# The last three even output tiles in two passes, latents first, and the odd norm's latent chain under the second

## The reference, cut to what matters

```python
for i in range(DEPTH):                                  # DEPTH = 2
    update_ctx = i < DEPTH - 1
    h_lat = rms_norm_2(x_lat, norm_g[i]) * (1.0 + sc_l) + sh_l
    h_ctx = rms_norm_2(x_ctx, norm_g[i]) * (1.0 + sc_c) + sh_c
    y_lat, y_ctx = even_mixer(h_lat, h_ctx, ...) if i == 0 else odd_mixer(h_lat, h_ctx, ...)
    x_lat = x_lat + g_l * y_lat
    if update_ctx:
        x_ctx = x_ctx + g_c * y_ctx
return rms_norm_2(x_lat, final_g)
```

## Time and profile before

| | |
|---|---|
| median of 3 runs | 2489.65 us |
| the profiled execution, its own time | 2498.05 us |
| its span | 2496.3 us |
| PE, DVE, ACT busy | 97%, 66%, 44% |
| chain that ended last | PE 86%, DVE 8%, ACT 3%, issue 2% |
| granted TensorE clock, mean of the span | 0.991 |

### The profile page before, as it was taken

The page is one execution under the profiler, slowest core; times in us unless marked ns, Lnnn a source line. Parts: engine busy times, 40 slices in busy tenths (PEclk is TensorE's granted clock), DMA queues, the critical chain, the costliest instruction groups (busy, mean ns, idle before and its releaser), DMA issues.

```text
span 2496.3 us, 36288 instructions
## 1 busy us (share of the span) xinstructions
PE 2423.2 (97%) x14094; PEld 1960.7 (79%) x14094; DVE 1655.3 (66%) x3206; ACT 1100.0 (44%) x2073; POOL 0.2 (0%) x4
## 2 busy tenths in 40 slices
PE   8999999999999999999999999999999999999998
PEld 6878888778888778788887888887866666878766
DVE  6767577474447776674865644488586677489765
ACT  4346355443232243464544423333446667242563
POOL 0000000000000000000000000000000000000000
PEclk9999999999999999999999999999999999999999
DMA  4320143223337522201522333465110000122211
GB/s 155 96 76 28 40 139 96 73 79 99 94 100 236 176 75 91 68 20 51 169 68 68 93 97 97 152 219 164 60 43 18 18 18 18 60 77 68 81 47 60
DMA packets 61802, 217.68 MB, mean 87 GB/s; under 512 B 6976, under 2 KB 9280, under 8 KB 60864
## 3 DMA queue, kind: packets, MB, share of 16 engines
q1 hardware_dynamic: 48384, 176.06, 22.8%
q10 hardware_dynamic: 13248, 39.29, 4.7%
HBM read 213.23 MB, written 2.10 MB: 86 GB/s over the span
## 4 chain that ended last, share of the span: by engine, by line
PE 86%; DVE 8%; ACT 3%; issue 2%; ACTq 0%; DMA 0%; DVEq 0%
PE bank L614 21%; PE bank L615 20%; PE bank L616 20%; PE bank L878 4%; PE bank L916 3%; PE bank L890 3%; DVE w_lo L576 2%; PE bank L645 1%; PE bank L647 1%; PE bank L646 1%; ACT w_hi L569 1%; PE bank L671 1%; DVE e_s L991 1%; PE bank L1522 1%; PE bank L673 1%
## 5 line engine op out<-in xcount | busy, mean ns | idle before, releaser
L569 ACT ACTIVATE w_hi<-w_raw 128x1024 fp32r<-128x1024 f32 x334 | 353.7, 1060 | 552.3 <-PE bank L616 505.8
L576 DVE TENSOR_TENSOR w_lo<-w_raw,w_hi 128x1024 fp32r<-128x1024 f32 x334 | 407.9, 1223 | 232.7 <-ACT w_hi L569 231.7
L614 PE MATMUL bank<-a_hi,w_hi 128*128 128x512 f32 x1344 | 535.0, 398 | 20.4 <-DVE w_lo L576 18.5
L616 PE MATMUL bank<-a_hi,w_lo 128*128 128x512 f32 x1344 | 526.1, 391 | 0.0
L615 PE MATMUL bank<-a_lo,w_hi 128*128 128x512 f32 x1344 | 525.7, 391 | 0.0
L614 PEld LDWEIGHTS bank<-a_hi,w_hi 128*128 128x128 f32 x1344 | 252.3, 188 | 83.0 <-issue 18.7
L616 PEld LDWEIGHTS bank<-a_hi,w_lo 128*128 128x128 f32 x1344 | 252.0, 188 | 55.7
L615 PEld LDWEIGHTS bank<-a_lo,w_hi 128*128 128x128 f32 x1344 | 252.5, 188 | 51.7 <-issue 1.0
L614 PE MATMUL bank<-b_hi,w_hi 128*128 128x512 f32 x440 | 182.5, 415 | 4.0 <-DVE w_lo L576 2.7
L615 PE MATMUL bank<-b_lo,w_hi 128*128 128x512 f32 x440 | 172.9, 393 | 0.0
L616 PE MATMUL bank<-b_hi,w_lo 128*128 128x512 f32 x440 | 172.3, 392 | 0.0
(11 more groups left out here) (465 smaller groups left out, 4412.0 us busy)
## 6 DMA issues: line engine op xcount, KB each, us to landing
w_raw<-w_tiles SPq DMA_DIRECT2D x334, 512.0 KB, 3.5
mod_raw<-mod_tiles ACTq DMA_DIRECT2D x48, 512.0 KB, 3.9
hT<-xT ACTq DMA_DIRECT2D x8, 256.0 KB, 5.9
m_in<-memT ACTq DMA_DIRECT2D x2, 1024.0 KB, 4.9
mod_cond<-cond_rows ACTq DMA_DIRECT2D x2, 1024.0 KB, 5.4
d_bias<-rpb_tiles ACTq DMA_DIRECT2D x16, 128.0 KB, 2.3
out<-hT ACTq DMA_DIRECT2D x8, 256.0 KB, 2.2
ctx_sq<-ctxT ACTq DMA_DIRECT2D x1, 1024.0 KB, 9.0
```

The lines of the kernel that those rows point to most:

```text
L569: act.activation(w_hi[:, t % SPLIT, :], w_raw[:, t % RAW, :], ACT.Copy).then_inc(sem("w_rounded"), 1)
L576: dve.tensor_tensor(w_lo[:, t % SPLIT, :], w_raw[:, t % RAW, :], w_hi[:, t % SPLIT, :].bitcast(f32), ALU.subtract).then_inc(sem("w_split"), 1)
L614: pe.matmul(o, wh, chunk(hi, k, n), start=k == 0, stop=False)
L616: mm = pe.matmul(o, wl, chunk(hi, k, n), start=False, stop=k == kc - 1)
```

## The change

`even_out_pe` makes tiles 0 to 4 as before. Then it makes tiles 5 to 7 in two passes over the same three weight tiles: first the latents of all three, then the context of all three, tile by tile. A weight tile is released at the end of its context part. In the second pass PE makes the latents' sum of squares (`last_ssq_pe`) behind the fifth step and the latents' row behind the tenth. The block between even output and odd input in `second_pe`, warm-ups included, is gone. The context's sum of squares now stands in `odd_in_pe` behind the seventh step of `cv1`, and its row behind the fifth step of `cl1`.

DVE makes the adds and sums of squares of the latents for all tiles, those of the context for tiles 0 to 4; then the latent inverse, the split of `cv0`, and the 8 latent chunks with the split of `cl0` behind chunk 1's place and that of `cv1` behind chunk 4's place; then the context's three adds and sums, two weight splits, the context inverse and all 8 context chunks. ACT has the same order.

The diff (the unchanged body of moved functions is cut):

```diff
-        def group_steps(pe, jobs, order, need, hold=False):
+        def group_steps(pe, jobs, order, need, hold=False, last=True):
...
-                    mm.then_inc(*book.tile_used(name, *key))
+                    mm.then_inc(*(book.tile_used(name, *key) if last else filled(name, *key)))
...
-                    blocks[0] += KC
+                    if last:
+                        blocks[0] += KC
...
         def even_out_pe(pe):
...
-            for c in range(2, KC):
+            for c in range(2, SPLIT_FROM):
                 product(pe, (0, c), both("e_y"))
+            order = [(k, j) for j in range(KC - SPLIT_FROM) for k in range(KC)]
+            for _ in group_steps(pe, [((0, c), both("e_y")[0]) for c in range(SPLIT_FROM, KC)], order, lambda k: (),
+                                 last=False):
+                pass
+            key = ("m2", 1, "lat")
+            for n, _ in enumerate(group_steps(pe, [((0, c), both("e_y")[1]) for c in range(SPLIT_FROM, KC)], order,
+                                              lambda k: ())):
+                if n == 4:
+                    last_ssq_pe(pe, key)
+                if n == 9:
+                    rstd_pe(pe, key, S)
+
+        SPLIT_FROM = KC - SPLIT
 
         def even_out_dve(dve):
             for c in range(KC):
+                even_add_dve(dve, PARTS[0], c)
+                if c < SPLIT_FROM:
+                    even_add_dve(dve, PARTS[1], c)
                     lo_after(dve, "e_y/lat", 0, c)
                 if c:
-                    odd_sum_dve(dve, c - 1)
-            odd_sum_dve(dve, KC - 1)
+                    square_add_dve(dve, ("m2", 1, "lat"), c - 1)
+                if 0 < c <= SPLIT_FROM:
+                    ctx_add_dve(dve, c - 1)
...
+        def even_last_dve(dve):
+            for c in range(SPLIT_FROM, KC):
+                even_add_dve(dve, PARTS[1], c)
+                if c > SPLIT_FROM:
+                    ctx_add_dve(dve, c - 1)
+            ctx_add_dve(dve, KC - 1)
...
         def odd_in_pe(pe):
...
-                    product(pe, (1,), both(name) if with_ctx else both(name)[:1],
-                            need=mod_ready(1, "ctx") if name == "dk0" else None)
+                    steps = product_steps(pe, (1,), both(name) if with_ctx else both(name)[:1],
+                                          need=mod_ready(1, "ctx") if name == "dk0" else None)
+                    for k, _ in enumerate(steps):
+                        if name == "cv1" and k == 6:
+                            ctx_ssq_pe(pe, 1)
+                        if name == "cl1" and k == 4:
+                            ctx_rstd_pe(pe, 1)
...
             even_out_pe(pe)
-            warm_pe(pe, 2, "m2", 1)
-            ssq_pe(pe, ("m2", 1, "lat"), S)
-            ctx_ssq_pe(pe, 1)
-            warm_pe(pe, 1, "m2_rstd", 1)
-            rstd_pe(pe, ("m2", 1, "lat"), S)
-            ctx_rstd_pe(pe, 1)
-            warm_pe(pe, 1, "odd_in")
             odd_in_pe(pe)
...
+        LAST_AFTER = {1: SPLIT_FROM + 1, 4: SPLIT_FROM + 2}
...
             rms_act(act, ("m2", 1, "lat"), S)
-            ctx_rms_act(act, 1)
-            hi_after(act, "e_y/lat", 0, KC - 1)
-            mod_high_act(act, 1, PARTS[0])
-            mod_high_act(act, 1, PARTS[1], 0, 2)
+            hi_after(act, "e_y/lat", 0, SPLIT_FROM)
+            mod_high_act(act, 1, PARTS[0], after=lambda c: c in LAST_AFTER and hi_after(act, "e_y/lat", 0, LAST_AFTER[c]))
+            for c in range(SPLIT_FROM, KC):
+                ctx_square1_act(act, c)
             for name, *_ in OJ[:2]:
                 hi_after(act, f"{name}/lat", 1)
-            mod_high_act(act, 1, PARTS[1], 2)
+            ctx_rms_act(act, 1)
+            mod_high_act(act, 1, PARTS[1])
             odd_in_act(act)
...
             inverse_dve(dve, ("m2", 1, "lat"), S)
-            ctx_inverse_dve(dve, 1)
-            lo_after(dve, "e_y/lat", 0, KC - 1)
-            mod_chunks_dve(dve, 1, PARTS[0])
-            mod_chunks_dve(dve, 1, PARTS[1], 0, 2)
+            lo_after(dve, "e_y/lat", 0, SPLIT_FROM)
+            mod_chunks_dve(dve, 1, PARTS[0], after=lambda c: c in LAST_AFTER and lo_after(dve, "e_y/lat", 0, LAST_AFTER[c]))
+            even_last_dve(dve)
             for name, *_ in OJ[:2]:
                 lo_after(dve, f"{name}/lat", 1)
-            mod_chunks_dve(dve, 1, PARTS[1], 2)
+            ctx_inverse_dve(dve, 1)
+            mod_chunks_dve(dve, 1, PARTS[1])
             taps = conformer_dve(dve)
```

More of the change, by code:

```diff
@@ L1985, in ctx_rstd_pe, with mod_high_act @@
                 .then_inc(*filled("rstd", "m2", i, "ctx"))
-        def mod_high_act(act, i, part, first=0, last=KC):
+        def mod_high_act(act, i, part, first=0, last=KC, after=None):
             p, _, sl, n, w = part
@@ L1993, in mod_high_act @@
                    .then_inc(*done("hi", i, p, c))
+                if after:
+                    after(c)
         def mod_tmp(i):
@@ L1998, in mod_tmp, with mod_chunks_dve @@
             return c_y[:, :, :].rearrange("p a b -> p (a b)")[:, :2 * (S + M)].rearrange("p (a b) -> p a b", a=2)
-        def mod_chunks_dve(dve, i, part, first=0, last=KC):
+        def mod_chunks_dve(dve, i, part, first=0, last=KC, after=None):
             p, _, sl, n, w = part
@@ L2400, in even_out_dve, with even_add_dve @@
-                if c < KC - 1:
+                even_add_dve(dve, PARTS[0], c)
+                if c < SPLIT_FROM:
+                    even_add_dve(dve, PARTS[1], c)
                     lo_after(dve, "e_y/lat", 0, c)
                 if c:
-                    odd_sum_dve(dve, c - 1)
-            odd_sum_dve(dve, KC - 1)
+                    square_add_dve(dve, ("m2", 1, "lat"), c - 1)
+                if 0 < c <= SPLIT_FROM:
+                    ctx_add_dve(dve, c - 1)
+        def even_add_dve(dve, part, c):
+            p, _, _, n, w = part
+            b = bank(dve, f"e_y/{p}", 0, c)
+            x = stream(p)[:, c, :n]
+            dve.scalar_tensor_tensor(out=x, in0=b[:, :n], scalar=mod[:, 0, 2 * KC + c, w:w + 1], in1=x,
+                                     op0=ALU.mult, op1=ALU.add).then_inc(*freed(f"e_y/{p}", 0, c, also=("h2", p, c)))
@@ L2414, in odd_squares_act, with ctx_square1_act, ctx_add_dve @@
                 act.activation(sq[:, c % 2, :], hT[:, c, :], ACT.Square).then_inc(*done("sq", "m2", 1, "lat", c))
[L2415 to L2423, removed]
+                if c < SPLIT_FROM:
+                    ctx_square1_act(act, c)
+        def ctx_square1_act(act, c):
+            act.wait_ge(*when("h2", "ctx", c))
+            if c >= 2:
+                act.wait_ge(*when("ctx_added", c - 2))
+            act.activation(spread[:, M * (c % 2):M * (c % 2) + M], cT[:, c, :], ACT.Square)\
+               .then_inc(*done("ctx_sq1", c))
+        def ctx_add_dve(dve, c):
             dve.wait_ge(*when("ctx_sq1", c))
```

## The result

The median is 2499.66 us over 20 runs against 2493.99 for the kernel before in the same comparison: a ratio of **1.0029, interval 1.0020 to 1.0038**. On 2494 that is +7.2 us, between +5.0 and +9.5. (The two medians alone differ by 5.67 us, 1.0023, which lies in that interval; two of the 20 runs before, at 2694.73 and 10239.09 us, are strays.) The change makes the kernel slower by about the 0.25% that the prediction's sum gave, and with 20 runs that is told from no change.

What follows compares the result with a forecast made beforehand. PE bounds the kernel, with DVE's queue a second bound right behind the hole. -3.3 at the group, +8.7 from there to `cl2` and +0.8 for the clock give +6.2 on 2489.65: 2495.9 us, 0.25% slower, range 2489 to 2501.

Steps and rivals of the forecast that it cites:

- T: The moment at which PE ends the latents of tile 7; forecast at 2173.5, 8.4 us earlier than 2181.89.
- rival 1: Context row is there when DVE asks for it (2202.4, not 2208.8): kernel ends 0.9 us earlier, 2488.8; chance 0.11.
- Rivals 2 and 3: 2: whole hole won, 6 to 8.4 us faster, chance 0.05. 3: half clock strikes more than once, +10.4 us, 0.22.
- The clock term: One half-clock stretch of 3.4 us on cl2 after the long pause: +0.8 us, bounded by 0 and +2.5.
- It is not given back: DVE sets the pace up to dk0, PE behind it, so cl2's +5.4 us lateness stays to the end.
- the noise term: From three runs between 2485.15 and 2494.2: about 0.3%, 7.5 us, is what a measurement tells from no change.
- Within 0.3%: 0.58: Chance given to a measured time within 0.3% of before; slower had 0.36, faster 0.06.
- the whole forecast case: The change ends +4 to +8 us slower, with one pause at cl2 and no other; chance 0.62.

Runs made afterwards that it cites:

- with the row early: The changed kernel with the context's sum of squares behind cv1's first step, its row behind the third, root and inverse ahead of two splits: 0.9999 (0.9987 to 1.0011).
- the run with PE kept busy: The changed kernel with nine 512-column warm-up matmuls ahead of cl2, in PE's idle time: ratio 1.0023 (1.0013 to 1.0034).
- the taps experiments: Convolution taps put off behind cl2's split: changed kernel 1.0023, kernel before 1.0016, changed with row early and late split 0.9984; taps spread: 0.9975 (that last kernel), 0.9995 (before).
- the mended change: The changed kernel with the context row early and cv1's weight split behind chunk 7: 0.9998 against the kernel before; with the taps spread as well, 0.9975.
- the changed kernel with the taps put off: The changed kernel, context row still late, with cl2's split ahead of the convolution and fewer taps early: ratio 1.0023 (1.0009 to 1.0036).

## Why the prediction was right or wrong

**What held, step by step.** With T = 2163.0 in the trace after: the sums began at T+1.8 (forecast T+1.8); the first split of the group at T+6.2 (2169.17; worked out as the first chunk's time less 1.14); PE left the pass at T+10.9 (T+11.1); the wait in the group was 1.96 us (2.2) and ended at T+19.6, as said; the group ended at T+25.3 (T+25.5); DVE waited 2.11 + 3.96 = 6.1 us for the context's row (some 6), began the context chunks at T+35.0 (T+35.3) and took 7.7 us for them (7.7); `cl2` started at T+51.2 (T+51.5) behind 8.70 us of idle time (8.9). DVE's low half was the releaser. The point from which rival 1 was to decide showed itself too: with the row early the change is not slower, 0.9999 (the 0.9 us that rival 1 would gain are too few to tell). Rivals 2 and 3 did not come: the profiled execution has one stretch of half clock, on `cl2`, as the forecast itself had, and none in the group or the pass. That a wait of 2 us in the group can bring one is seen in the run with PE kept busy.

In the seam the terms came out as -4.0 up to the group's end (forecast -3.3), +8.6 from there to `cl2` (+8.7) and +1.05 for the clock (+0.8): +5.7 against +6.2.

**The clock term was a little under-sized.** I took +0.8 from one stretch of 3.4 us as in the earlier trace rows. The stretch lasted 9.7 us; it began inside the pause, so only 4 us of it fell on `cl2`: 18.36 - 17.31 = +1.05. In other kernels with a pause there it cost up to +2.0 (19.31), still under the bound of +2.5. The Trainium skill, "TensorE: Matmul & The Clock Gate", Part 1, has the throttled state as the default; the row at 2208.40 agrees for a pause of this length.

**"It is not given back" was right.** I had PE set the pace behind `dk0`. It does: 93.09 us to the first scores against 93.22 before (2330.10 - 2236.88), and from there to the end 166.2 us in both. Of the seam's +5.7, +5.5 is left at the end. My working did not look at DVE there, and was lucky in that. The score row lies 3.0 us behind the scores in the kernel before, on PE's and on DVE's timeline:

```profile
2330.10 1.14 PE L878 MATMUL bank<-d_k,d_q 64*128 64x256 f32 x8 [1.23 <-issue]
```

```profile
2333.14 0.69 DVE L991 CUSTOM_DVE_ANT_0 d_s<-bank,d_bias 128x512 f32<-128x512 f32 x1
```

In the kernel after it is 2.1 (2327.75 - 2325.64), and the rest of the span behind the row is longer by the same 0.9. So a lag of this size decides nothing. That DVE's lag does decide when it grows to 10 us, only the taps experiments show.

**The step that failed** is the noise term, "about 0.3%, 7.5 us, is what a measurement tells from no change", and with it "Within 0.3%: 0.58", the leaning to no change that was built on it. The mechanism and the sum hold: +6.2 lies within the measured +5.0 to +9.5, and 2499.66 lies in the range. But I took the scatter of three single runs for what a median of many can tell, and put a forecast of 0.25% under it, so that 0.46 of the forecast's 0.62 went to no change. Twenty runs a side gave an interval of ±0.09% (1.0020 to 1.0038): a slowdown of 0.29% is under my bound and yet three times that. The chance of slower should have been that of the whole forecast case: the sign was better known than the size.

The same three runs gave the base of the forecast time. Their median, 2489.65 us, is 4.3 below the 2493.99 of twenty runs, and that is more than the whole 3.8 us by which 2495.9 fell short of 2499.66.

## What to carry to other kernels

A hole on the busiest engine is worth filling only if the queue that feeds the next tile delivers earlier too: here DVE held the next tile's weight split behind context work, and the hole came back some 33 us later at nearly its old length. When small work is put off, look for the next place where its engine is the only one that can go on. Here that was the first score row: 2 to 3 us behind PE's scores it cost nothing, 10 us behind them 6.6 to 6.9. Measure a part of a change in the old kernel as well as in the new one: the order of the context work alone cost 0.35%, and the mended change was worth 5 us once DVE's queue no longer stood in its way. Three runs are too few to say what a measurement can tell.

## What the runs showed of the hardware

Pauses of the same length, in the same code, met different clocks. Behind 1.96 us of waiting in the group the granted clock stayed at 1.00 in the kernel after and in the run with the row early; behind 1.97 us it was 0.54 for 3.4 us in the run with PE kept busy, and behind 1.95 us 0.53 for 3.4 us in the changed kernel with the taps put off (2184.0 to 2187.4). Why these short ones differ stays open: a pause of 2.11 us before `cl2` in that same run was followed by 1.00.

Behind the longer pauses before `cl2` it fell to half in all five kernels that had one, but the longer pause did not cost more. Pauses of 8.7 us were followed by 18.36, 19.02 and 19.16 us from `cl2` to `dk0`, pauses of 3.72 and 5.07 us by 19.31 and 19.19, all against 17.31. In the first of them the clock was down at 2208.4, 2.9 us into the pause, and up again some 4 us after PE had begun; the part of it that lay in the pause cost nothing.

Two executions may reach the same place, behind the same code, 10 us apart (2146.64 and 2156.66, at tile 5), more than the whole effect measured here; one span less another says nothing at this size.
